# A streaming encoder's two layers on one core: four gate chunks by high and low parts, and an earlier order around the sample's attention and the experts' first quad

## The chip, the cores and the metric

The kernel runs on one core of one Trainium2 chip. The metric is the device time of a launch in microseconds, here the median of three runs. Profiles are single executions; their times count from the first instruction.

## What is computed

Two layers over 288 tokens of 1024 features in fp32: 256 of a prompt and 32 of a sample with a cache of earlier keys. Of each layer (cut):

```python
z = x @ w_in                       # [rnn | q | k | v | rnn gate | attn gate]
y_rnn = rglru(conv(z_rnn))         # linear recurrence over the tokens
o = attention(rope(q), rope(k), v) # banded for the prompt, cache for the sample
merged = sigmoid(z_gr) * (y_rnn @ w_br_rnn) + sigmoid(z_ga) * (o @ w_br_attn)
x = layernorm(alpha * x + merged @ w_out)
eidx, gate = route(x)              # 8 of 64 experts for each token
x = layernorm(alpha * x + shared(x) + sum(gate_e * expert_e(x)))
```

## The kernel before, in words

Activations lie with features on partitions (8 groups of 128, `xT`), tokens along the free dimension. The product with `w_in` goes by chunks of 128 output features; two chunks share a weight piece of 1 MB. A chunk is made in one of two ways. `over_features` (L563, matmuls L569) multiplies fp32 by fp32, 8 matmuls of 288 columns, two records each in the trace. `over_parts` (L572) has both operands split into a high and a low part of a reduced fp32 type and adds three products for each of 8 groups (L582, L583, L584), 24 matmuls. The low times low product is left out. The parts of activations are made once; those of a weight piece are made by ScalarE (`high_parts`, L1069: two copies into `whi`, which has two buffers) and VectorE (`low_parts`, L1409: two subtractions into `dense_lo`). `SPLIT` lists the pieces that are treated so, in order. Pieces go through a ring of three slots (`dense`); SyncE asks for piece d when piece d-3 is used, and puts transfers of the first quad's expert weights between them (`EXPERTS_AFTER`).

Work items are numbered (`Z_RNN` to `Z_FILL2`). Items before the gates use six PSUM banks in turn, from the gates on two. Each has two semaphores by parity: `z_ready`, set by TensorE, and `z_free`, set when the item was read out. `bank_of` (L555) waits before TensorE writes an item's bank: an item from the gates on waits until all earlier items of its parity are free.

TensorE's order in a layer: 8 chunks of the recurrence's input; k and v; 8 query chunks (items 10, 13, ..., 31), each with two block products of the recurrence's gates (L695; items 32 and 33 belong to the last). ScalarE turns the halves of each query chunk (L1129, four copies) and applies two sigmoids (L1153); VectorE makes the rotation (L1504, L1505, L1507). Behind query chunks 1 and 3 both also make parts of later pieces. Then come 16 gate chunks (items 34 to 49), spread over the attention by hand:

- `GATES_AHEAD`: chunk 0; transposes of the last keys and the sample's scores (L722 to L735); chunk 1; the sample's transposes (L743, L744), which wait for its softmax; the first pair's scores (L713, L714); chunks 2 and 3; the sample's output (L756, L757), which waits for ScalarE's copies of the transposed probabilities; chunk 4.
- `GATES_WITH`: for each of 8 pairs of heads, scores of the next pair, gate chunks, output of the pair before (`pair_output`, L771 to L773), transposes of this pair's probabilities (L791).

The chunks 0 to 7 go by `over_features` (pieces 9 to 12), 8 to 15 by `over_parts` (pieces 13 to 16). ScalarE reads each chunk out with a Tanh (`keep_gates`, L1162). Between, ScalarE makes the sample's exponentials (L1169), eight Exp (L1177) and eight Tanh (L1182) for the recurrence, the copies of the sample's probabilities (L1188, L1189), one Sqrt (L1193, a table load before and one after), and the exponentials of a pair (L1203). VectorE: maxima of the sample's scores (L1541), the product of gate and input (L1548), the sample's normalisation (L1534), squares (L1553, L1554), masked scores of the first pair (L1562 to L1566), memsets and the product and scan of the recurrence (L1573 to L1579), then the first pair's normalisation (L1534).

After the layer norm, the routed experts go in 16 quads of four. Before the first quad's turning TensorE makes the shared expert's last product (`shared_down`, L871, 8 chunks in two banks) and waits until VectorE has added its last chunk (L1792). Then come the turning of the hidden values (L920), slots to tokens (L942), and the gather of the next quad (L892 to L895), which needs the next one-hot matrix (L1722, VectorE). VectorE makes that behind the last sum.

## Time and profile before

| what | value |
|---|---|
| median of 3 runs | 1590.09 us (1589.77 to 1591.45) |
| profiled execution, its own time | 1589.3 us |
| its span | 1587.5 us |
| TensorE matmul busy | 1550.0 us (98%) |
| TensorE weight load busy | 1034.5 us (65%) |
| VectorE, ScalarE busy | 741.5 us (47%), 573.9 us (36%) |
| granted TensorE clock, mean | 0.997 |
| HBM read | 474.88 MB, 300 GB/s over the span |

A busy TensorE is one with a matmul under way, not one at its peak. The layers are alike: layer 0's gates lie at 82 to 175 us, its experts at 285 to about 800, layer 1's gates at 866 to 956, its experts from 1069 on. A row of an order of time has the start, the duration (of a merged group, from its first start to its last end), engine, line, operation, tiles, partitions x elements, count, and in brackets how long the engine had been idle and who released it.

### The profile page before, as it was taken

What the parts mean: (1) busy time and instruction counts of PE and PEld (TensorE: products, weight loads), DVE (VectorE), ACT (ScalarE), POOL (GpSimd) and SP (SyncE); (2) the same over time, 40 slices, a digit from 0 to 9 for tenths busy, and PEclk for the clock granted to TensorE, in tenths of its full rate; (3) what the DMA queues carried; (4) which work ended last, traced back from release to release, by engine and by line L of the source; (5) the groups of instructions that cost most, each with busy time, mean ns of one, the idle gap of its engine ahead of it and who ended that gap; (6) DMA issues with size and microseconds to landing.
All of it is one profiled execution on the core that took longest, in us unless ns stands there. A gap on an engine that the chain in (4) does not pass through costs nothing.

```text
span 1587.5 us, 25312 instructions
## 1 busy us (share of the span) xinstructions
PE 1550.0 (98%) x9446; PEld 1034.5 (65%) x9446; DVE 741.5 (47%) x1513; ACT 573.9 (36%) x1108; POOL 25.0 (2%) x40
## 2 busy tenths in 40 slices
PE   7999999999999999999999999999999999999996
PEld 7968997655655565555598699975565555556554
DVE  5768667332433333233474776562243333324335
ACT  5756433222232232223267664342223223222322
POOL 2000000000000000000010000000000000000000
PEclk9999999999999999999999999999999999999998
DMA  8552446599999999999546424458999999999991
GB/s 235 188 209 85 134 160 245 212 372 409 410 399 402 401 417 401 403 404 402 206 127 232 153 91 153 147 212 322 401 404 398 408 404 416 400 404 407 401 407 45
DMA packets 141557, 477.38 MB, mean 301 GB/s; under 512 B 10020, under 2 KB 74084, under 8 KB 108724
## 3 DMA queue, kind: packets, MB, share of 16 engines
q1 hardware_dynamic: 139728, 473.50, 77.0%
q0 software_dynamic: 1408, 2.85, 0.7%
q8 instruction: 44, 0.72, 0.2%
q10 hardware_dynamic: 356, 0.13, 0.0%
q14 instruction: 21, 0.17, 0.0%
HBM read 474.88 MB, written 1.57 MB: 300 GB/s over the span
## 4 chain that ended last, share of the span: by engine, by line
PE 92%; DVE 5%; ACT 2%; issue 1%; DMA 0%; SPq 0%; DVEq 0%; ACTq 0%
PE ps L910 28%; PE ps L933 14%; PE ps L582 6%; PE ps L583 6%; PE ps L584 6%; PE ps L569 6%; PE ps L954 4%; PE ps L955 4%; PE ps L893 4%; PE ps L892 4%; PE ps L895 2%; PE ps L942 1%; PE ps L871 1%; PE ps L920 1%; PE ps L1004 1%
## 5 line engine op out<-in xcount | busy, mean ns | idle before, releaser
L910 PE MATMUL ps<-experts,xg 128*64 128x512 f32 x2048 | 445.0, 592 | 0.0
L910 PEld LDWEIGHTS ps<-experts,xg 128*64 128x64 f32 x2048 | 146.9, 137 | 291.5 <-issue 290.6
L582 PE MATMUL ps<-parts 128*128 128x288 f32 x768 | 232.4, 303 | 1.1 <-DVE dense_lo L1409 0.4
L933 PE MATMUL ps<-experts,hid 128*64 128x512 f32 x1024 | 226.8, 595 | 0.4 <-ACT hid L1283 0.4
L584 PE MATMUL ps<-parts,dense_lo 128*128 128x288 f32 x768 | 226.1, 294 | 0.0
L1749 DVE SCALAR_TENSOR_TENSOR yl<-ps,gsl,yh 128x512 fp32r<-128x512 f32 x128 | 96.1, 751 | 254.8 <-ACT yh L1291 254.8
L1737 DVE TENSOR_TENSOR hid<-ps,hid 128x256 f32<-128x256 f32 x64 | 27.2, 425 | 378.6 <-ACT hid L1278 378.6
L1278 ACT ACTIVATE hid<-ps 128x256 f32<-128x256 f32 x64 | 24.6, 385 | 404.8 <-PE ps L910 404.8
L933 PEld LDWEIGHTS ps<-experts,hid 128*64 128x64 f32 x1024 | 71.6, 137 | 131.9 <-issue 127.9
L1270 ACT ACTIVATE xg<-ps,gperm_all 128x256 f32<-128x256 f32 x256 | 130.8, 562 | 71.5 <-PE ps L895 71.5
L582 PEld LDWEIGHTS ps<-parts 128*128 128x128 f32 x768 | 144.3, 188 | 4.8 <-issue 2.3
L584 PEld LDWEIGHTS ps<-parts,dense_lo 128*128 128x128 f32 x768 | 144.5, 188 | 0.0
L892 PE MATMUL ps<-oh,xh 128*128 128x256 f32 x512 | 136.4, 288 | 0.0
L1291 ACT ACTIVATE yh<-ps,gsl 128x512 fp32r<-128x512 f32 x128 | 88.1, 688 | 128.8 <-PE ps L933 128.8
L893 PE MATMUL ps<-oh,xl 128*128 128x256 f32 x512 | 133.5, 282 | 0.0
L954 PE MATMUL ps<-ohT,yh 128*128 128x288 f32 x480 | 132.2, 305 | 0.0
L955 PE MATMUL ps<-ohT,yl 128*128 128x288 f32 x480 | 129.1, 295 | 0.0
L1409 DVE TENSOR_TENSOR dense_lo<-dense,parts 128x1024 fp32r<-128x1024 f32 x96 | 113.2, 1221 | 19.4 <-ACT parts L1069 19.4
L569 PE MATMUL ps<-xT,dense 128*128 128x288 f32 x448 | 112.6, 409 | 4.4 <-ACT B L1153 2.7
L1756 DVE TENSOR_TENSOR ffT<-ps,ffT 128x288 f32<-128x288 f32 x240 | 109.6, 456 | 15.4
L583 PE MATMUL ps<-parts 128*128 128x288 f32 x384 | 113.3, 295 | 0.0
L1069 ACT ACTIVATE parts<-dense 128x1024 fp32r<-128x1024 f32 x96 | 96.1, 1052 | 42.3 <-PE ps L584 41.7
(287 smaller groups left out, 1964.0 us busy)
## 6 DMA issues: line engine op xcount, KB each, us to landing
experts<-in_w SPq DMA_DIRECT2D x384, 1024.0 KB, 10.0
dense<-in_w_in SPq DMA_DIRECT2D x34, 1024.0 KB, 5.5
dense<-in_w_br_rnn SPq DMA_DIRECT2D x8, 1024.0 KB, 5.3
dense<-in_w_br_attn SPq DMA_DIRECT2D x8, 1024.0 KB, 5.2
dense<-in_w_out SPq DMA_DIRECT2D x8, 1024.0 KB, 5.2
dense<-in_ws SPq DMA_DIRECT2D x6, 1024.0 KB, 5.5
tok<-in_x_prompt SPq DMA_DIRECT2D x1, 1024.0 KB, 5.7
out_y_prompt<-tok SPq DMA_DIRECT2D x2, 512.0 KB, 2.6
```

The costliest lines, as they stand in the source:

```text
L569: last = mm(bank[:, 0:n], w[:, k, col:col + P], rhs(k), start=k == 0, stop=k == KC - 1)
L582: mm(bank[:, 0:T], w_hi[:, k, col:col + P], hi[:, k, :], start=k == 0, stop=False)
L583: mm(bank[:, 0:T], w_hi[:, k, col:col + P], lo[:, k, :], start=False, stop=False)
L584: last = mm(bank[:, 0:T], w_lo[:, k, col:col + P], hi[:, k, :], start=False, stop=k == KC - 1)
L892: mm(o, xh[:, t, x], oh[:, t, :], start=t == 0, stop=False)
L893: mm(o, xl[:, t, x], oh[:, t, :], start=False, stop=False)
L910: last = mm(ps[e % 2 * CAP:(e % 2 + 1) * CAP, UP[u], :], xg[:, k, e * CAP:e * CAP + CAP], experts[:, e, 0:2, k * DE:k * DE + DE], start=k ...
L933: last = mm(ps[e % 2 * CAP:(e % 2 + 1) * CAP, DOWN[u][b], :], hidT[:, u, m, e % 2 * CAP:(e % 2 + 1) * CAP], experts[:, e, 2, m * D + b * 5 ...
L954: mm(o, yh[:, u, c * P:c * P + P], ohT[:, u, :], start=u == 0, stop=False)
L955: last = mm(o, yl[:, u, c * P:c * P + P], ohT[:, u, :], start=False, stop=u == 1)
L1270: last = activation(xg[:, k, :], ps[:, SWAP[j], k % 2 * 256:k % 2 * 256 + 256], ACT.Identity, bias=gperm_all[:, L, 1, k:k + 1], scale=gper ...
L1409: V.tensor_tensor(low[:, x], slot[:, x], as_f(whi[:, f % 2, x]), ALU.subtract).then_inc(wlo_ready, 1)
```

## The change

Pieces 9 and 10 (`D_G`, `D_G + 1`) join `SPLIT`, so gate chunks 0 to 3 go by parts too. ScalarE and VectorE make their parts behind query chunks 5 and 7. Chunk 2 moves from behind the sample's transposes to ahead of them. Chunk 0 waits for item 30, the last one in its own bank, and no longer for item 32. ScalarE keeps chunk 0 ahead of the sample's exponentials, chunk 1 behind them, chunk 2 behind the eight Exp. The last chunk, 15, is made in two halves: groups 0 to 3 before the output of pair 6, groups 4 to 7 behind the transposes of pair 7, and it is kept behind the copies of pair 7's probabilities. Behind the shared expert, the wait for the last sum moves behind turning and slots to tokens (`shared_added`), and VectorE makes quad 1's one-hot before the eight sums.

```diff
--- before.py
+++ after.py
@@ -97,7 +97,7 @@
 RING = 3
 
 
-SPLIT = list(range(D_IN + 1, D_KV + 1)) + list(range(D_Q, D_G)) + list(range(D_G + 4, D_ROUTER))
+SPLIT = list(range(D_IN + 1, D_KV + 1)) + list(range(D_Q, D_G + 2)) + list(range(D_G + 4, D_ROUTER))
 F_Q = SPLIT.index(D_Q)
 F_G = SPLIT.index(D_G + 4)
 F_BR = SPLIT.index(D_BR)
@@ -110,7 +110,7 @@
 EXPERTS_AFTER = (D_G, D_G + 2, D_G + 4, D_ROUTER + 2, D_ROUTER + 2, D_ROUTER + 2)
 
 
-GATES_AHEAD = ((0, 1), (2, 3), (4,))
+GATES_AHEAD = ((0, 1, 2), (3,), (4,))
 
 GATES_WITH = ((5, 6), (7,), (8,), (9, 10), (11,), (12, 13), (14,), (15,))
 H_WITH = 2
@@ -558,7 +558,10 @@
 
                 if Z_DEEP <= i < Z_GATE:
                     pe.wait_ge(z_free[i % 2], z_count(L, i - Z_DEEP) + 1)
-                elif i >= Z_GATE:
+                elif i == Z_GATE:
+
+                    pe.wait_ge(z_free[i % 2], z_count(L, Z_GATE - Z_GATE % Z_DEEP) + 1)
+                elif i > Z_GATE:
                     pe.wait_ge(z_free[i % 2], z_count(L, i))
                 return ps[:, z_bank(i), :]
 
@@ -569,12 +572,12 @@
                     last = mm(bank[:, 0:n], w[:, k, col:col + P], rhs(k), start=k == 0, stop=k == KC - 1)
                 return last
 
-            def over_parts(L, bank, d, col, hi, lo, ready=None):
+            def over_parts(L, bank, d, col, hi, lo, ready=None, ks=range(KC)):
 
                 f = SPLIT.index(d)
                 w_hi = whi[:, f % 2, :].rearrange("p (k c) -> p k c", k=KC)
                 w_lo = dense_lo[:, d % RING, :].rearrange("p (k c) -> p k c", k=KC)
-                for k in range(KC):
+                for k in ks:
                     if col == 0 and k % 4 == 0:
                         pe.wait_ge(wlo_ready, (L * len(SPLIT) + f) * 2 + (k // 4 + 1))
                     if ready:
@@ -695,7 +698,7 @@
                         mm(bank_of(L, i)[:, 0:U], wax[:, j, c, :], u_[:, c, :], start=True, stop=True).then_inc(z_ready[i % 2], 1)
                 def gate_chunks(ms):
                     for m in ms:
-                        if m >= KC:
+                        if D_G + m // 2 in SPLIT:
                             over_parts(L, bank_of(L, Z_GATE + m), D_G + m // 2, m % 2 * P, x_hi, x_lo).then_inc(z_ready[m % 2], 1)
                             continue
                         if m % 2 == 0:
@@ -773,6 +776,12 @@
                         last = mm(ps[lo:hi, 6, 0:P], v[:, 0, kv], pt[:, 2 * P:3 * P], start=True, stop=True)
                     last.then_inc(s_o, 1)
 
+                def last_gate(ks):
+                    m = 2 * KC - 1
+                    if ks[0] == 0:
+                        bank_of(L, Z_GATE + m)
+                    return over_parts(L, ps[:, z_bank(Z_GATE + m), :], D_G + m // 2, m % 2 * P, x_hi, x_lo, ks=ks)
+
                 for c in range(KC):
                     n = L * (KC + 1) + c + 1
 
@@ -780,7 +789,10 @@
                         gate_chunks(GATES_WITH[c])
                     if c < KC - 1:
                         pair_scores(c + 1)
-                    if c > 0:
+                    if c == KC - 1:
+                        last_gate(range(KC // 2))
+                        pair_output(c - 1)
+                    elif c > 0:
                         gate_chunks(GATES_WITH[c][:1])
                         pair_output(c - 1)
                         gate_chunks(GATES_WITH[c][1:])
@@ -790,6 +802,7 @@
                         for k in range(3):
                             last = transpose(ps[:, 4 + h, k * P:k * P + P], S[:, c % 2, h, k * P:k * P + P], ident)
                     last.then_inc(s_pT, 1)
+                last_gate(range(KC // 2, KC)).then_inc(z_ready[(2 * KC - 1) % 2], 1)
                 pair_output(KC - 1)
 
 
@@ -870,6 +883,8 @@
                         for m in range(ME):
                             last = mm(bank[:, 0:T], w[:, m, c * P:c * P + P], hs[:, m, :], start=m == 0, stop=m == ME - 1)
                         last.then_inc(z_ready[c % 2], 1)
+
+                def shared_added():
                     for b in range(2):
                         pe.wait_ge(z_free[b], z_count(L, Z_SH2 + KC))
 
@@ -955,7 +970,7 @@
                             last = mm(o, yl[:, u, c * P:c * P + P], ohT[:, u, :], start=False, stop=u == 1)
                         last.then_inc(c_full, 1)
 
-                def quad(n, first=False, last=False):
+                def quad(n, first=False, last=False, after=None):
                     if not first:
                         up(n, 0)
                         up(n, 1)
@@ -963,6 +978,8 @@
                     turn(n)
                     slots_to_tokens(n, 0)
                     slots_to_tokens(n, 1)
+                    if after:
+                        after()
                     if not last:
                         gather(n + 1, n)
                     down(n, 0)
@@ -974,7 +991,7 @@
                     up(q, 1)
                     if meanwhile:
                         meanwhile()
-                    quad(q, first=True)
+                    quad(q, first=True, after=shared_added if meanwhile else None)
                     with pe.Fori(1, NQUAD - 1) as i:
                         quad(q + i)
                     if meanwhile:
@@ -1152,7 +1169,7 @@
                         bank = z_item(L, i)
                         activation(dst[:, c, :], bank[:, 0:U], ACT.Sigmoid, bias=prm_all[:, L, b * KC + c:b * KC + c + 1])\
                             .then_inc(z_free[i % 2], 1)
-                    if c in (1, 3):
+                    if c % 2:
                         high_parts(L, F_Q + 2 + c // 2)
                 def keep_gates(ms):
 
@@ -1162,6 +1179,8 @@
                         activation(dst, bank[:, 0:T], ACT.Tanh, scale=0.5).then_inc(z_free[m % 2], 1)
 
 
+                act.wait_ge(xc_used, L + 1)
+                keep_gates(GATES_AHEAD[0][:1])
                 act.wait_ge(s_max, L * (KC + 1) + 1)
                 for h in range(2):
                     for a in range(2):
@@ -1169,14 +1188,14 @@
                         activation(S[:, 0, h, a * 160:a * 160 + 160], ps[:, 2 + h, a * 160:a * 160 + 160], ACT.Exp,
                                    bias=ats[:, 0, 1, x:x + 1], scale=SCALE, accum_out=ats[:, 0, 2, x:x + 1])
                 activation(ats[:, 0, 4, :], ats[:, 0, 3, :], ACT.Exp).then_inc(s_exp, 1)
+                keep_gates(GATES_AHEAD[0][1:2])
                 act.wait_ge(gxu, L + 1)
                 for b in range(2):
                     act.wait_ge(z_free[b], z_count(L, Z_GATE))
                 act.wait_ge(decay_set, 1)
                 for c in range(KC):
                     activation(a_[:, c, :], gl_[:, c, :], ACT.Exp, scale=c8[:, 0, L, c:c + 1]).then_inc(act_own, 1)
-                act.wait_ge(xc_used, L + 1)
-                keep_gates(GATES_AHEAD[0])
+                keep_gates(GATES_AHEAD[0][2:])
                 act.wait_ge(act_own, (L + 1) * KC)
                 for c in range(KC):
                     activation(gl_[:, c, :], gl_[:, c, :], ACT.Tanh, scale=c8[:, 1, L, c:c + 1]).then_inc(a_and_t, 1)
@@ -1217,12 +1236,14 @@
                         keep_gates(GATES_WITH[c])
                     if c < KC - 1:
                         exponentials(c + 1)
-                    if c > 0:
+                    if 0 < c < KC - 1:
                         keep_gates(GATES_WITH[c])
                     act.wait_ge(s_pT, n + 1)
                     act.wait_ge(s_o, L * (KC + 1) + max(c, 1))
                     activation(PTa[:, w, 0, :], ps[:, 4, 0:3 * P], ACT.Copy)
                     activation(PTa[:, w, 1, :], ps[:, 5, 0:3 * P], ACT.Copy).then_inc(s_pT_kept, 1)
+                    if c == KC - 1:
+                        keep_gates(GATES_WITH[c])
                     if c in HIGH_WITH:
                         high_parts(L, F_G + HIGH_WITH.index(c))
 
@@ -1512,7 +1533,7 @@
                         decay_rates()
                     if L == 0 and c == 5:
                         sink_tables()
-                    if c in (1, 3):
+                    if c > 0 and c % 2:
                         low_parts(L, F_Q + 2 + c // 2)
                 dve.wait_ge(out_rows, 2 * L + 1)
                 V.tensor_copy(k_rows[:, 0, :], ps[:, 7, 0:P])
@@ -1755,11 +1776,11 @@
                         dve.wait_ge(c_full, FREE + n * KC + (c + 1))
                         V.tensor_tensor(ffT[:, c, :], ps[:, SWAP[c % len(SWAP)], 0:T], ffT[:, c, :], ALU.add).then_inc(c_added, 1)
 
-                def quad(n, i, first=False, last=False, hidden_made=False):
-                    if not last:
+                def quad(n, i, first=False, last=False, made=False):
+                    if not last and not made:
                         dve.wait_ge(og_ready, n + 1)
                         one_hot(n + 1, i + 1)
-                    if not hidden_made:
+                    if not made:
                         hidden(n, 0)
                         hidden(n, 1)
                     if not first:
@@ -1786,6 +1807,8 @@
                         V.tensor_tensor(hs[:, m, :], ps[:, 6 + m, 0:T], hs[:, m, :], ALU.mult).then_inc(sh_hid, 1)
                     hidden(q, 0)
                     hidden(q, 1)
+                    dve.wait_ge(og_ready, q + 1)
+                    one_hot(q + 1, 1)
 
                     for c in range(KC):
                         bank = z_item(L, Z_SH2 + c)
@@ -1803,7 +1826,7 @@
                     gated(q, 0)
                     if first:
                         meanwhile()
-                    quad(q, 0, first=True, hidden_made=first)
+                    quad(q, 0, first=True, made=first)
                     with dve.Fori(1, NQUAD - 1) as i:
                         quad(q + i, i)
                     V.tensor_scalar(rank[:, :, :], rank[:, :, :], -float(CAP), None, ALU.add).then_inc(next_round, NQUAD)
```


## Rows read from the trace of the kernel before

**Rows 1.** TensorE's waits over the span: total us, times, longest us

```profile
PE ps L569 <- ACT B L1153: 2.7, 2, 1.4
PE ps L743 <- DVE S L1534: 2.5, 2, 1.3
...
PE ps L920 <- DVE ffT L1792: 1.5, 2, 0.8
```

**Rows 2.** TensorE in order of time, layer 1: start, duration, [idle before <-releaser]

```profile
865.97 4.12 PE L569 MATMUL ps<-xT,dense 128*128 128x288 f32 x16 [1.37 <-ACT B L1153]
...
871.48 4.15 PE L569 MATMUL ps<-xT,dense 128*128 128x288 f32 x16
876.89 0.33 PE L743 MATMUL ps<-cst,S 128*128 128x128 f32 x1 [1.27 <-DVE S L1534]
...
879.59 8.00 PE L569 MATMUL ps<-xT,dense 128*128 128x288 f32 x32 [0.74 <-ACT B L1162]
```

**Rows 3.** Order of time, layer 1, last pair, TensorE and VectorE

```profile
955.11 0.43 PE L771 MATMUL ps<-PTa,v 128*64 128x128 f32 x2 [0.96 <-ACT PTa L1225]
...
949.04 1.01 DVE L1534 TENSOR_SCALAR S<-S,ats 128x256 f32<-128x256 f32 x4
```

**Rows 4.** Chain that ended last, layer 1, gate chunks 4 to 6

```profile
890.46 11.84 PE ps L569 x48
```

**Rows 5.** A stretch, L582 alone: PE busy (x), PEld busy (x), clock

```profile
957.00:989.00 32.00, 23.80 (x81) 15.03 (x81) 1.00 0.41 133
```

**Rows 6.** Order of time, layer 0, one piece's high and low parts

```profile
68.35 2.00 ACT L1069 ACTIVATE parts<-dense 128x1024 fp32r<-128x1024 f32 x2
...
69.51 2.36 DVE L1409 TENSOR_TENSOR dense_lo<-dense,parts 128x1024 fp32r<-128x1024 f32 x2 [0.79 <-ACT parts L1069]
```

**Rows 7.** SyncE's DMA issues in order of time, layer 1

```profile
855.32 8.71 SPq L446 DMA_DIRECT2D dense<-in_w_in  x2
```

**Rows 8.** The page's DMA issues: count, KB each, median us to landing

```profile
dense<-in_w_in SPq DMA_DIRECT2D x34, 1024.0 KB, 5.5
```

**Rows 9.** ScalarE in order of time, layer 1

```profile
863.66 1.64 ACT L1129 ACTIVATE tmp<-ps 32x288 f32<-32x288 f32 x4 [1.34 <-PE ps L584]
...
865.99 0.50 ACT L1153 ACTIVATE B<-ps,prm_all 128x291 f32<-128x291 f32 x1 [0.15 <-DVE qT L1504]
...
875.61 3.54 ACT L1177 ACTIVATE B<-B,c 128x291 f32<-128x291 f32 x8 [0.80 <-DVE B L1548]
...
879.63 3.53 ACT L1182 ACTIVATE B<-B,c 128x291 f32<-128x291 f32 x8
883.06 0.37 ACT L1188 ACTIVATE PTa<-ps 128x256 f32<-128x256 f32 x1
```

**Rows 10.** VectorE in order of time, layer 1

```profile
871.59 0.89 DVE L1541 TENSOR_REDUCE ats<-ps 128x2 f32<-128x320 f32 x2 [0.69 <-PE ps L735]
...
872.99 2.58 DVE L1548 TENSOR_TENSOR B<-B 128x2328 f32<-128x2328 f32 x1
...
891.56 0.07 DVE L1573 MEMSET B<- 128x8 f32 x1 [1.86 <-ACT B L1193]
...
900.45 1.01 DVE L1534 TENSOR_SCALAR S<-S,ats 128x256 f32<-128x256 f32 x4
```

**Rows 11.** Order of time, layer 0, VectorE and TensorE

```profile
78.36 0.46 DVE L1504 TENSOR_TENSOR qT<-ps,cst 128x288 f32<-128x288 f32 x1
...
82.65 0.48 PE L569 MATMUL ps<-xT,dense 128*128 128x288 f32 x1 [1.37 <-ACT B L1153]
```

**Rows 12.** Order of time, layer 1, shared expert, TensorE and VectorE

```profile
1083.06 8.03 PE L871 MATMUL ps<-hs,dense 128*128 128x288 f32 x32
...
1084.33 0.46 DVE L1792 SCALAR_TENSOR_TENSOR ffT<-xT,ps 128x288 f32<-128x288 f32 x1 [0.32 <-PE ps L871]
...
1091.76 0.96 DVE L1722 TENSOR_TENSOR oh<-cst,rank 128x768 fp32r<-128x768 f32 x1 [0.19 <-DVE ffT L1792]
```

**Rows 13.** The span's end: busy PE, PEld, DVE, ACT, POOL; clock, DMA

```profile
1576.00:1587.50 11.50, 0.00 (x0) 0.00 (x0) 8.72 (x14) 2.06 (x3) 0.00 (x0) 0.57 0.27 103
```

## The prediction, made before the change was run

> **What bounds the kernel now.** I read the waits of TensorE first, then its order of time in layer 1, then ScalarE and VectorE beside it, then the same places of layer 0. TensorE is the bound: it waits for others for a few microseconds only, and the places that the change touches are among them [rows 1]: the first gate chunk behind a sigmoid (2.7 us over both layers), the sample's transposes behind its softmax (2.5), the first token work of the experts behind a sum (1.5). Layer 1 adds 0.74 us in front of gate chunk 2 [rows 2] and 0.96 in front of the last pair's output [rows 3]. So an instruction taken from TensorE, or a wait taken away, counts in full, as long as ScalarE and VectorE keep up.
>
> **Part 1, four chunks split.** A gate chunk by fp32 takes 11.84/3 = 3.95 us (the stretch of chunks 4 to 6) [rows 4]. A chunk by parts is 24 matmuls, 8 of them of L582; 81 of these in 32.0 us [rows 5] make 0.395 us for each three and 3.2 us for a chunk. So 0.75 us a chunk, 3.0 a layer. That time comes from the rows. The Trainium skill (FP8 and Floating Point Precision, TensorE Precision Notes) says that a true fp32 matmul goes through the array in four passes; three passes would then be 2.96 us, and the eight chunks together would give 1.9 us more than by my rows. This case's rows have 0.81 of the fp32 time, not 0.75, and the sum goes by them.
>
> The price is paid by ScalarE, 2.00 us of high parts for each of two weight pieces, and VectorE, 2.36 us of low parts, the second half ending 3.5 us after ScalarE's begin [rows 6]. They lie behind query chunks 5 and 7. The later of the two pieces (10) is asked for at 855.32 in layer 1 and read by ScalarE from 866.4 on, 11 us later, where such a transfer lands in 5.5 us as a median [rows 7, 8]; so I put no wait there.
>
> **Part 2, the start and the front, layer 1.** The chunk at 865.97 waits 1.37 us for the sigmoid of chunk 7. By the new rule it needs the second one of chunk 6, over before the rotation of chunk 7 begins, so it follows L695 at once, at 864.5 (865.97 - 1.37, a tenth less for overlap). ScalarE has 1.34 us of idle time before the rotation of chunk 7 [rows 9], which takes the delay by the first high parts (0.6 us there). The chunk ends at 867.7; kT's transposes and the sample's scores, 1.5 us (871.48 - 865.97, less 4.0 for the chunk) [rows 2], end at 869.2, 2.3 us earlier than now.
> Then the second high parts: they begin 0.4 us after the sigmoid of 865.99, at 866.4, and VectorE's low parts end at 869.9 [rows 6, 9]. Behind them on VectorE are queued the copy of the key rows (0.5 us) and the sample's maxima. These begin at 870.3 for 871.59; the wait for scores has become one for low parts. Everything of that chain is 1.3 us earlier: gx·u begins at 871.7 for 872.99 [rows 10], and ScalarE's eight exponentials at 874.3. Between these and the eight Tanh it now keeps one gate chunk and not two (0.3 us), so the Tanh begin 1.6 us earlier, at 878.05, and the copies of the sample's probabilities 1.6 earlier, at 881.45 [rows 9]. Four of them take 1.2 us, so TensorE can multiply them at 882.65.
> TensorE meanwhile: chunks 1 and 2 from 869.2 to 875.6; transposes and first pair's scores 875.6 to 877.6 (876.89 to 878.85 now, L743 to the wait before 879.59) [rows 2]; chunk 3 to 880.8. The waits of 1.27 and 0.74 us are gone, and a **new one of 1.85 us** stands before the sample's output, 882.65. Its 2.9 us (879.59 + 8.00 to 890.46) and chunks 4 to 6 with 11.84 follow unchanged [rows 2, 4]: 902.3 becomes 897.5. **Gain 4.8 us.**
> Next on the path could be the first pair's softmax. Today its last multiplication ends at 901.46, 9.9 us behind the memset at 891.56 [rows 10], which waits for a Sqrt that waits for gate chunk 3. With chunk 3 kept early, the Sqrt waits only for VectorE's squares, which move with the Tanh, 1.6 us; the masked scores before the memset end at 888.1, and the softmax at 898.0. TensorE wants it at 897.5 + 0.9 = 898.4. So it is hidden, by 0.4 us only. If the table load before Sqrt (1.3 us) can't start ahead of the wait, 0.5 us a layer is lost.
>
> **The same in layer 0.** VectorE also sets the sink tables behind query chunk 5, until chunk 6's product with cosine at 78.36 [rows 11]. The low parts begin there and end at 80.65, and that product waits for them. ScalarE's sigmoid ends at 81.6, and the first gate chunk begins at 81.75 for 82.65 [rows 11]: 0.9 us for the 1.5 above. Its last sigmoid ends at 84.5 for 83.16, the high parts at 86.4, the low parts at 87.85, and gx·u begins at 89.7, as today. So the Tanh gains just the 0.3 us of one chunk less; TensorE resumes with the sample's output at 100.65 instead of 104.2. **Gain 3.5 us**, and the margin before the softmax is 0.4 us again, since the Sqrt no longer waits for a gate chunk.
>
> **Part 3, the last chunk in halves.** Today TensorE stands for 0.96 us between the transposes (end 954.15) and the last pair's output [rows 3]. Half a chunk, 1.6 us, now lies there and covers ScalarE's two copies (0.5 us each). The total of TensorE's work stays. The transposes come 1.6 us earlier and need the last softmax at 951.6; its multiplications end by 950.05 today [rows 3]. ScalarE's keeping of chunk 15 and the high parts behind it come later against the work, yet o's high and low parts end at 961.1, and piece 18 is due at 961.9. The piece that waits for chunk 15's slot is due 14 us later. **Gain 0.96 a layer, 1.9.**
>
> **Part 4, the one-hot ahead of the sums.** The 0.75 us before L920 [rows 1] goes: turning and slots run while the last sum is added, and the gather's wait is met behind them. But VectorE now makes the one-hot, 0.96 us [rows 12], between the hidden products and the first sum, which moves from 1084.33 to 1084.9 and ends at 1085.35, while TensorE wants that bank at 1085.1 (two chunks of 8.03/8 = 1.0 us behind 1083.06). That is a new wait of 0.3 to 0.4 us. **Gain 0.4 a layer, 0.8**; the ends are 0 and 0.75.
>
> **Sum.** 4.8 + 3.5 + 1.9 + 0.8 = 11.0 us. The experts' stage has no wait of TensorE for a weight and only moves. The profiled execution takes 1589.3 us, which would be 1578.3. The median of the runs stands 0.8 us above it, so the same gain gives **1579.1 us**.
>
> **Bounds.** Upwards in gain: layer 0 like layer 1 (+1.3) and no stall in part 4 (+0.7): 1577.1; another microsecond if the chain to the Tanh is a little shorter: 1576. Downwards: 0.5 a layer for the table load, a microsecond a layer on the ScalarE and VectorE chains (nothing in the trace shows high parts between Sigmoid and the sample's Exp), none of part 4: 1.0 + 2.0 + 0.8 = 3.8, 1583. The instructions of part 2 on TensorE can't cost less than their rows.
>
> **Rivals.**
> *The helpers' chain sets the front* (chance 0.20). If ScalarE and VectorE slip by 2 to 3 us in each front, because copies and subtractions are in the way of rotations and sigmoids as in layer 0's decay rates, the new wait grows from 1.85 to 4 or more and half the front's gain (4.2) is gone: 1579.1 + 4.2 = 1583.3. For it: the margins before the first pair's softmax are 0.4 us. Against it: ScalarE has 1.34 us to spare before a rotation in layer 1 [rows 9].
> *The parts come late* (0.05). The chunk waits for piece 9 or 10, which were not read before so early; a transfer later by 4 to 5 us in each layer would eat the 8.3 of the front and leave 2.7: 1587.4, within 0.2% (what a measurement of this kernel can tell from no change, 3.2 us). Against it: piece 10 is asked for 11 us before use [rows 7].
> *The clock falls in the new wait* (0.03). This is the one that ends slower. In the last 11.5 us, where TensorE is idle, the granted clock is 0.57 [rows 13]; today waits of 1.4 us leave it at 1.00. The new wait of 1.85 us is the longest inside the layers, with transposes close before it. If the clock went to 1.2 of 2.4 GHz there and came back only at the end of chunk 6, the 14.8 us of work after it [rows 4] would take 14.8 more in each layer: 29.6 - 11.0 = 18.6 slower, 1608.7. It decides from 7.1 us a layer on ((11.0 + 3.2)/2). The Trainium skill speaks for this direction (TensorE: Matmul & The Clock Gate, HAM oscillation): short bursts with waits between them send the array back to half clock each time. The trace so far agrees only at the end of the kernel, and disagrees around every wait inside it, so the chance is small.
> *It does not do what it says* (0.02): the halves or the early start change nothing because another count of the same semaphore holds; only part 1 stays, 6.0 less the new wait's 3.7: 1587.8.
>
> **How the numbers follow.** My forecast has 0.70. The range takes its bounds and the nearer half of the first rival: 1576 to 1583.5. Faster by over 0.2%: the forecast and the first rival, 0.90; within it the late parts and the change without effect, 0.07; slower the clock, 0.03.
>
> **What would show it.** Right: L569's first wait gone and layer 1's gate chunk within 0.2 us of L695; a wait of about 1.8 us before L756, with ScalarE as releaser; no wait before the last L771; L920 straight behind L871 and a wait of 0.3 inside L871; L1548 at the same time as before in layer 0 and 1.3 us earlier in layer 1. Wrong: a wait for L1534 behind chunk 6, one of L582 for low parts in the first gate chunks, or a granted clock below 1.00 between the layers' fronts and chunk 6.

## The result, and the profile after

Five runs of the kernel after have a median of **1580.72 us** (1580.43 to 1584.69), five of the kernel before beside them 1590.09 (1588.79 to 1591.45): a ratio of 0.9945, 95% interval 0.9931 to 0.9960. It is faster by 9.4 us. The forecast was 1579.1 in a range of 1576.0 to 1583.5; 11.0 us of gain were expected. The profiled execution took 1580.72 us itself, with a span of 1578.8.

The span's start varies by some microseconds between executions (the wait for the sample's input alone is 7.1 to 8.6 us). So I compare a stretch behind it: from the block products of query chunk 4 in layer 0, at 66.55 here, to the first quad's turning in layer 1, at 1083.17. I call it the **stretch**. It was 1024.9 us before and is 1016.6 after, 8.3 less; with 0.4 us from its start that is the whole difference of the spans, 8.7.

First the waits of TensorE over the span of the kernel after (total us, times, longest us). The three rows of before [rows 1] are gone but for 0.3 us before the sample's transposes and 0.5 us before the first gate chunk, both in layer 0. In their place stands a new one, ahead of the sample's output.

```profile
PE ps L599 <- DMA tok<-in_x_sample: 7.4, 1, 7.4
PE ps L759 <- ACT PTa L1208: 3.6, 2, 1.8
...
PE ps L585 <- ACT B L1170: 0.5, 1, 0.5
...
PE ps L746 <- DVE S L1555: 0.3, 1, 0.3
```

TensorE in order of time, layer 1: start, duration, and in brackets the idle time and who ended it. The first gate chunk stands directly behind the block products and no longer waits [rows 2], chunks 1 and 2 take 6.5 us, and the sample's transposes wait for nothing.

```profile
859.66 1.14 PE L698 MATMUL ps<-B,wax 128*128 128x291 f32 x4
860.42 0.51 PE L585 MATMUL ps<-parts 128*128 128x288 f32 x1
...
865.37 0.40 PE L585 MATMUL ps<-parts 128*128 128x288 f32 x1
...
871.87 0.27 PE L746 MATMUL ps<-cst,S 128*128 128x128 f32 x1
...
873.70 0.40 PE L585 MATMUL ps<-parts 128*128 128x288 f32 x1
...
878.88 0.40 PE L759 MATMUL ps<-PTa,vc_all 128*64 128x128 f32 x2 [1.72 <-ACT PTa L1208]
```

The chain that ended last has gate chunks 4 to 6 behind that, in layer 0 and in layer 1. They took 11.84 us before [rows 4].

```profile
103.26 13.53 PE ps L572 x48
...
881.80 13.51 PE ps L572 x48
```

The same 48 records are 1.7 us longer. Why, the windows of layer 0 show (start:end, us, then busy time and count of PE, PEld, DVE, ACT, POOL, the granted clock, DMA share, GB/s): TensorE is busy throughout, and its granted clock is 0.53 in the third one.

```profile
96.00:100.00 4.00, 2.50 (x19) 2.26 (x17) 3.27 (x5) 4.00 (x12) 0.00 (x0) 1.00 0.10 9
100.00:103.30 3.30, 2.97 (x17) 1.62 (x18) 3.16 (x5) 2.07 (x4) 0.00 (x0) 1.00 0.97 328
103.30:106.70 3.40, 3.40 (x8) 2.44 (x9) 3.19 (x11) 3.12 (x2) 0.00 (x0) 0.53 1.03 405
106.70:110.00 3.30, 3.30 (x14) 2.52 (x14) 3.23 (x3) 0.94 (x4) 0.00 (x0) 0.97 0.50 200
```

In layer 1 the window 882.0 to 885.3 has 0.52. In the same place before, every window has 1.00; this one is of layer 1:

```profile
890.50:902.30 11.80, 11.80 (x50) 9.00 (x50) 9.65 (x15) 4.94 (x13) 0.00 (x0) 1.00 0.84 299
```

ScalarE and VectorE, layer 1, in order of time. The table load of L1212 begins behind the kept chunk, 2.5 us before its Sqrt, and the first pair's last multiplications end at 894.07.

```profile
879.05 1.28 ACT L1212 ACT_TABLE_LOAD   x1
881.55 2.14 ACT L1212 ACTIVATE B<-B 128x2328 f32<-128x2328 f32 x1 [1.22 <-DVE B L1575]
```

```profile
867.80 2.58 DVE L1569 TENSOR_TENSOR B<-B 128x2328 f32<-128x2328 f32 x1
...
893.06 1.01 DVE L1555 TENSOR_SCALAR S<-S,ats 128x256 f32<-128x256 f32 x4
```

Last, the end of the attention and the shared expert, TensorE in layer 1. The last pair's output follows the second half of chunk 15 with no wait, where 0.96 us stood before [rows 3], and the turning L935 stands directly behind the shared product, which is 8.33 us long for 8.03 [rows 12].

```profile
947.06 0.43 PE L774 MATMUL ps<-PTa,v 128*64 128x128 f32 x2
...
1075.00 8.33 PE L884 MATMUL ps<-hs,dense 128*128 128x288 f32 x32
1083.17 0.60 PE L935 MATMUL ps<-cst,hid 128*128 128x128 f32 x4
```

Cut at the same points, the two traces give (us, layer 0 / layer 1):

| stretch | before | after | difference |
|---|---|---|---|
| block products of chunk 4 to the sample's output | 37.25 / 36.55 | 33.79 / 31.72 | -3.46 / -4.83 |
| to the second pair's scores | 14.72 / 14.72 | 16.38 / 16.36 | +1.66 / +1.64 |
| to the last pair's output | 52.88 / 52.88 | 51.83 / 51.82 | -1.05 / -1.06 |
| to the first quad's first product | 114.06 / 114.06 | 114.05 / 114.05 | 0 |
| to the turning | 22.65 / 22.68 | 22.05 / 22.05 | -0.60 / -0.63 |

The turning of layer 0 to chunk 4 of layer 1, 542.5 us, is the same in both.

### The profile page after: what moved, and what is told of

Read it like the earlier page. It is cut to its first block, busy times and chain, and to the rows that moved or that the text cites. A ratio compares the mean times of both kernels' runs of the same rounds, so it can differ in the third digit from the quotient of the medians.

```text
span 1578.8 us, 25460 instructions
## 1 busy us (share of the span) xinstructions
PE 1548.1 (98%) x9510; PEld 1038.9 (66%) x9510; DVE 750.7 (48%) x1521; ACT 581.1 (37%) x1116; POOL 25.0 (2%) x40
## 4 chain that ended last, share of the span: by engine, by line
PE 90%; DVE 5%; ACT 2%; issue 1%; DMA 0%; SPq 0%; DVEq 0%; ACTq 0%
PE ps L925 28%; PE ps L948 14%; PE ps L585 6%; PE ps L586 6%; PE ps L587 5%; PE ps L969 4%; PE ps L572 4%; PE ps L970 4%; PE ps L907 4%; PE ps L908 4%; PE ps L910 2%; PE ps L957 1%; PE ps L884 1%; PE ps L935 1%; DVE dense_lo L1430 1%
## 5 line engine op out<-in xcount | busy, mean ns | idle before, releaser
L585 PE MATMUL ps<-parts 128*128 128x288 f32 x832 | 252.1, 303 | 1.5 <-ACT B L1170 0.5
L587 PE MATMUL ps<-parts,dense_lo 128*128 128x288 f32 x832 | 244.9, 294 | 0.0
L585 PEld LDWEIGHTS ps<-parts 128*128 128x128 f32 x832 | 156.3, 188 | 6.1 <-issue 2.2
L587 PEld LDWEIGHTS ps<-parts,dense_lo 128*128 128x128 f32 x832 | 156.5, 188 | 0.0
L1430 DVE TENSOR_TENSOR dense_lo<-dense,parts 128x1024 fp32r<-128x1024 f32 x104 | 122.6, 1221 | 23.3 <-ACT parts L1086 23.2
L586 PE MATMUL ps<-parts 128*128 128x288 f32 x448 | 132.2, 295 | 0.0
L1086 ACT ACTIVATE parts<-dense 128x1024 fp32r<-128x1024 f32 x104 | 104.0, 1051 | 42.4 <-PE ps L587 36.2
L969 PEld LDWEIGHTS ps<-ohT,yh 128*128 128x128 f32 x480 | 90.2, 188 | 24.3 <-issue 24.3
```

What stands on the lines that cost most here:

```text
L585: mm(bank[:, 0:T], w_hi[:, k, col:col + P], hi[:, k, :], start=k == 0, stop=False)
L586: mm(bank[:, 0:T], w_hi[:, k, col:col + P], lo[:, k, :], start=False, stop=False)
L587: last = mm(bank[:, 0:T], w_lo[:, k, col:col + P], hi[:, k, :], start=False, stop=k == KC - 1)
L969: mm(o, yh[:, u, c * P:c * P + P], ohT[:, u, :], start=u == 0, stop=False)
L1430: V.tensor_tensor(low[:, x], slot[:, x], as_f(whi[:, f % 2, x]), ALU.subtract).then_inc(wlo_ready, 1)
```

## The experiments

Diffs are against the kernel after unless said otherwise. "Front" is the first line of the table above, "tail" the second, which holds the small products of the sample's output (2.9 us) and gate chunks 4 to 6.

### The clock behind the wait

The theory: the clock falls because TensorE stands idle for 1.8 us. The rival: the products by parts ahead of it count for less. First, useless products fill the wait (`keep_clock`, a helper that both kernels use at two other places; here two fp32 products of 512 columns of a constant, into the bank that the sample's output overwrites next).

```diff
                 gate_chunks(GATES_AHEAD[1])
+                keep_clock(6, 2)
```

> The changed kernel with two fp32 products of 128x512 without use (about 0.85 us each) in the new wait before the sample's output; nothing else. Theory A: the granted clock fell to 0.50 for 3.4 us in each layer because TensorE stood 1.84 us. Then the clock stays at 1.00, chunks 4 to 6 take 11.84 us again and not 13.5, and the time is 1.7 us a layer less: about 1577.3 us. Theory B: the clock falls for another cause (the small products of the sample's output, or the products by parts ahead of them). Then it falls as before and the time stays at 1580.7 us.

Measured: 1578.41 us (1577.34 to 1580.55, 5 runs), ratio to before 0.9928 (0.9914 to 0.9941). The stretch is 1013.3, 3.3 less than after, and the front is the same within 0.05 us: the fillers (1.88 us) lie where the wait was. The windows of its layer 0:

```profile
98.20:100.20 2.00, 1.94 (x6) 0.63 (x4) 1.93 (x3) 2.00 (x8) 0.00 (x0) 1.00 0.27 32
100.20:103.10 2.90, 2.82 (x16) 1.51 (x16) 2.76 (x5) 1.67 (x3) 0.00 (x0) 1.00 1.02 353
103.10:115.00 11.90, 11.90 (x51) 9.07 (x50) 11.52 (x21) 5.94 (x13) 0.00 (x0) 1.00 0.67 242
```

So the fall hangs on the wait, and it costs 3.3 us in this execution. One filler leaves 1.0 and 0.9 us of the wait:

```diff
+                keep_clock(6, 1)
```

> The changed kernel with one useless product of 0.85 us in the wait instead of two; about 1.0 us of wait is left. Theory A, by the kernel before, whose waits of 1.37 us left the clock at 1.00: no fall, chunks 4 to 6 take 11.84 us, S is 1013.3 as with two. Rival: a wait of any length behind small products is enough, the clock falls and S is 1016.6.

1582.71 us (1580.46 to 1584.61, 4 runs), ratio 0.9945 (0.9927 to 0.9964), stretch 1016.4. The clock fell again, in both layers (layer 0):

```profile
103.00:107.00 4.00, 3.03 (x18) 1.53 (x17) 3.83 (x6) 2.76 (x7) 0.00 (x0) 0.95 0.91 279
107.00:110.50 3.50, 3.50 (x9) 2.56 (x9) 3.29 (x11) 3.08 (x2) 0.00 (x0) 0.56 1.03 407
```

That is a miss for length as the cause: before, waits of 1.37 and 1.27 us leave the clock at 1.00, and in split_only below one of 2.66 us does. The next kernel makes the wait longer, without new products by parts: pieces 9 and 10 by fp32, chunk 3 behind the wait.

```diff
-SPLIT = list(range(D_IN + 1, D_KV + 1)) + list(range(D_Q, D_G + 2)) + list(range(D_G + 4, D_ROUTER))
+SPLIT = list(range(D_IN + 1, D_KV + 1)) + list(range(D_Q, D_G)) + list(range(D_G + 4, D_ROUTER))
-GATES_AHEAD = ((0, 1, 2), (3,), (4,))
+GATES_AHEAD = ((0, 1, 2), (), (3, 4))
```

with `c in (1, 3)` in both helpers as before.

> No chunk of the first four by parts (as in no_split), and gate chunk 3 moved behind the sample's output, so that a wait of some 2.3 us stands there again though no product by parts is new. Stretch S from the block products of query chunk 4 in layer 0 to the first quad's turning in layer 1: 1024.9 us before, 1016.6 changed, 1013.8 no_split. Theory A (the wait makes the clock fall): it falls in both layers, S is 1013.8 + 4.6 of waits + 3.4 of slow clock, 1021.8. Rival (products by parts make it fall): the clock stays at 1.00 and S is 1018.4.

1593.81 us (1589.7 to 1597.14, 10 runs), ratio 1.0022 (1.0010 to 1.0034), stretch 1026.2: slower than before. The wait is 3.3 us in each layer, and the clock is at half for twice as long:

```profile
97.50:100.80 3.30, 2.21 (x8) 1.05 (x8) 3.16 (x5) 2.22 (x5) 0.00 (x0) 0.70 0.00 0
100.80:104.50 3.70, 3.70 (x12) 2.07 (x12) 3.46 (x12) 3.23 (x2) 0.00 (x0) 0.50 0.01 2
104.50:108.00 3.50, 3.50 (x14) 2.69 (x13) 3.43 (x3) 0.20 (x1) 0.00 (x0) 0.84 0.00 0
```

The expectation was missed by 4.4 us: with 2.3 us of wait and 1.7 of slow clock a layer, the stretch was to be 1021.8. The waits are 1.0 us longer each, and the slow clock costs 2.9 and 3.0. The profiled execution is the fastest of the ten; the others have a mean granted clock of 0.993 down to 0.991, so the loss in them is as large or larger.

The rival is out as a condition: the clock falls without a single new product by parts, if behind a longer wait than in the kernel after. And in layer 0 the half clock already begins at 98.8, only 0.2 us behind the start of the sample's output (98.58): 0.70 over the first window is 2.0 us at half. So there the small products behind the wait can't be what brought the clock down.

Two kernels keep the wait out of the place by real work. In the one, gate chunk 4 goes ahead of the sample's output:

```diff
+                gate_chunks(GATES_AHEAD[2])
                 pe.wait_ge(s_pT_kept, L * (KC + 1) + 1)
...
-                gate_chunks(GATES_AHEAD[2])
```

> The changed kernel with gate chunk 4 ahead of the sample's output, so that real work lies in the new wait. Theory A: no wait of TensorE and no fall of the clock there; of the 3.5 us a layer that this frees (1.84 of wait, 1.7 of slow clock) the first pair's softmax lets about 2.1 through and takes the rest as a wait behind chunk 6 of 1.3 us: about 1576.4 us. Theory B (clock falls for another cause): the fall remains, and the time is 1.8 us a layer less at most, with no wait for the softmax: 1577 to 1578 us.

1578.85 us (1576.41 to 1579.80), ratio 0.9922 (0.9909 to 0.9936), stretch 1012.1, no wait before the output and the clock at 1.00. But it gives back 1.3 and 1.2 us: the first pair's transposes now wait 1.4 to 1.5 us for its softmax, as the row of its waits shows (two of the four are the 0.5 us that every kernel here has at a later pair):

```profile
PE ps L802 <- DVE S L1554: 3.8, 4, 1.5
```

The other keeps the wait, where it was, and makes chunk 4 between the wait and the sample's output:

```diff
                 pe.wait_ge(s_pT_kept, L * (KC + 1) + 1)
+                gate_chunks(GATES_AHEAD[2])
...
-                gate_chunks(GATES_AHEAD[2])
```

> The kernel after, but TensorE waits for the last sample's kept probabilities (s_pT_kept) first, then makes gate chunk 4 (dense, 3.9 us), and only then the small products of the sample's output. The wait of about 1.84 us stays at its place in the order; what stands right behind it is dense work in place of the 2.9 us of small products. Theory C (the clock falls where a wait stands directly beside the small products of the sample's output, and they fill the time behind it): the granted clock stays at 1.00, chunks 4 to 6 take their 11.84 us of work in place of 13.5, nothing is lost behind the wait, the stretch from layer 0's fifth block group to layer 1's first turning is 1013.3 us (1016.6 less 3.3), and the time some 1577.5 to 1579.5. Rival (a wait of 1.84 us at this place is enough, whatever follows): the wait is 1.8 again, the clock falls to 0.50 for 3.4 us or more in both layers, the stretch is 1016.6 (1018 to 1020 where it is low for 6.8 us), the time 1580.5 to 1584.5 as for the kernel after.

1579.84 us (1577.88 to 1581.18, 5 runs), ratio 0.9933 (0.9920 to 0.9947), stretch 1013.6. The wait is there and the clock does not fall. First TensorE's row, then the windows of layer 0:

```profile
101.55 4.12 PE L572 MATMUL ps<-xT,dense 128*128 128x288 f32 x16 [1.79 <-issue]
```

```profile
99.70:101.60 1.90, 0.10 (x2) 0.08 (x1) 1.83 (x3) 1.90 (x7) 0.00 (x0) 1.00 0.37 33
101.60:105.70 4.10, 4.10 (x17) 2.98 (x18) 3.93 (x7) 2.86 (x3) 0.00 (x0) 1.00 1.03 370
105.70:108.60 2.90, 2.90 (x17) 1.53 (x18) 2.73 (x9) 2.87 (x6) 0.00 (x0) 1.00 1.03 410
```

A wait of the same length at the same moment, the same small products 4 us later, and 3.0 us are saved. So, for a wait of this length, it is neither the wait nor the small products alone, but the two side by side. That rests on two fronts in one trace, and on the mean granted clocks below.

### What the split is worth

Without the two pieces (`SPLIT` and the helpers as before, the order of the kernel after kept):

> The changed kernel with pieces 9 and 10 left as one fp32 product each, so gate chunks 0 to 3 take 3.95 us again; start, order, halves and one-hot stay. Theory A: four times 0.75 us more work fill the wait before the sample's output, the clock stays at 1.00, and without parts the helpers start 0.3 to 1.3 us earlier. The front then gains 3.8 us in each layer against the kernel before, and the time is 1578 us: the split of four chunks is worth nothing or less. Rival (what the prediction's sum said, no clock): the split is worth 3.0 us a layer less the wait of 1.85, so without it the time is 1 to 2 us more than 1580.7: 1582 to 1583 us.

1579.20 us (1578.92 to 1582.09), ratio 0.9932 (0.9919 to 0.9946), stretch 1013.8: **less than with the split**, by 2.8 us. TensorE has some 5.4 us more to do (in layer 1 the front less its waits is 32.67 us for 30.0, so 2.7 a layer and not the 3.0 of the rows), and no wait stands before the sample's output. The front is 33.37 / 32.67, so 0.4 shorter in layer 0 and 0.95 longer in layer 1; the rest is the clock, which stays at 1.00.

The split alone, on the kernel before (pieces 9 and 10 in `SPLIT`, `D_G + m // 2 in SPLIT`, parts behind all odd query chunks):

> The kernel before with the four chunks by parts and nothing else (order, start, last chunk and one-hot as before). By rows 3.0 us a layer less work. Theory A: ScalarE's and VectorE's chain holds back the sample's transposes, a wait of 2 to 3 us stands before them, and only 2.4 us of layer 1 and 1.6 of layer 0 arrive; if the clock falls behind these waits, 1.7 a layer goes again. S 1020.9 to 1024.3 of 1024.9. Rival (the prediction's term as it stands): S 1018.9.

1588.23 us (1586.26 to 1589.58, 10 runs), ratio 0.9985 (0.9975 to 0.9994), stretch 1021.8, 3.1 less than before. Of the 5.4 us by which TensorE's work is shorter, 2.6 come back as longer waits at the two first places of [rows 1]:

```profile
PE ps L582 <- ACT B L1153: 3.9, 2, 2.7
PE ps L743 <- DVE S L1534: 3.9, 2, 2.0
```

And the clock: in layer 1, where the second of these waits stands at 876.99 (1.95 us) and another 0.64 us at 879.58, it is 1.00 in every window. In layer 0 it is 1.00 as well, around waits of 2.66 us (before the first gate chunk, by parts), 1.96 and 0.65.

```profile
872.00:880.00 8.00, 5.41 (x42) 4.71 (x41) 4.76 (x12) 6.01 (x20) 0.79 (x2) 1.00 0.70 250
880.00:889.00 9.00, 9.00 (x63) 7.51 (x62) 7.98 (x12) 7.29 (x16) 0.00 (x0) 1.00 0.16 37
```

Only piece 9 split, in the order of the kernel after:

```diff
-... list(range(D_Q, D_G + 2)) ...
+... list(range(D_Q, D_G + 1)) ...
-                    if c % 2:
+                    if c in (1, 3, 5):
```

> The changed kernel with piece 9 split (gate chunks 0 and 1) and piece 10 not. Theory A: TensorE needs 1.5 us more than with four chunks by parts, so the wait before the sample's output shrinks to 0.3 us or nothing and the clock stays at 1.00; gain of the front 5.2 us in layer 1 and 4.7 in layer 0: about 1576 us. Rival (no cost of the clock in the wait): the work of 1.5 us fills the wait and the time stays at 1580.7 us.

1579.36 us (1577.18 to 1580.21), ratio 0.9932 (0.9918 to 0.9945), stretch 1012.0: the shortest with chunk4_ahead. TensorE does not wait before the sample's output (0.48 us stand before layer 0's first gate chunk), and yet that output begins earlier than in the kernel after (front 32.74 / 31.29). The reason is on VectorE: without the low parts of piece 10 its product of gate and input begins 21.17 / 19.72 us behind the block products of chunk 4, for 22.71 / 20.64 after. VectorE and TensorE (layer 1):

```profile
864.66 2.58 DVE L1569 TENSOR_TENSOR B<-B 128x2328 f32<-128x2328 f32 x1
```

```profile
849.10 1.14 PE L698 MATMUL ps<-B,wax 128*128 128x291 f32 x4
...
876.23 0.43 PE L759 MATMUL ps<-PTa,vc_all 128*64 128x128 f32 x2
```

### The three other parts, each undone

The first gate chunk waits for item 32 again (`elif i >= Z_GATE`, no case of its own):

> The changed kernel, but gate chunk 0 again waits for all earlier items of its parity (the sigmoid of query chunk 7). Theory A: TensorE starts 0.9 us later in layer 0 and 1.5 later in layer 1, the wait before the sample's output shrinks by as much to under 1 us, the output itself moves by 0 and 0.5 us, and the clock does not fall: S is 1016.6 - 3.4 + 0.5 = 1013.7, so the early start costs more than it brings here. Rival (no tie of the clock to the wait): S is 1017.1, or 1019.0 where the start was on the path in full.

1583.77 us (1582.79 to 1584.17, 4 runs), ratio 0.9954 (0.9937 to 0.9970), stretch 1017.7. The front is 34.41 / 32.36, so the early start is worth 0.62 and 0.64 us. The expected stretch was 1013.7, with no fall of the clock behind so short a wait; that is missed. The wait before the sample's output is 0.8 us in both layers. In layer 0 the clock holds (tail 14.69), in layer 1 it falls, for twice as long as after, and the tail is 17.94:

```profile
881.00:884.40 3.40, 3.40 (x17) 1.71 (x17) 3.26 (x6) 2.18 (x2) 0.00 (x0) 0.79 0.86 280
884.40:888.00 3.60, 3.60 (x8) 2.60 (x9) 3.39 (x10) 2.53 (x2) 0.00 (x0) 0.50 1.05 408
```

The last gate chunk whole, as before:

```diff
-                    if c == KC - 1:
-                        last_gate(range(KC // 2))
-                        pair_output(c - 1)
-                    elif c > 0:
+                    if c > 0:
-                last_gate(range(KC // 2, KC)).then_inc(z_ready[(2 * KC - 1) % 2], 1)
```

> The changed kernel with the last gate chunk in one piece ahead of pair 6's output and kept where it was. By theory and by the prediction's part 3 the wait of 0.96 us before the last pair's output is back in both layers and S grows by 1.9 to 2.1 us to 1018.6. Rival: the halves only moved the wait (into the transposes of pair 7 or into the branch products), S grows by under 1 us.

One run, 1587.26 us (before beside it 1591.53), stretch 1020.1. The part up to the last pair's output is 52.86 in both layers for 51.83: the halves are worth **1.05 us a layer**. The other 1.4 us are the clock's: with the same instructions in the front, it fell for twice as long in layer 1 (tail 17.83).

The wait for the last sum and the one-hot as before:

```diff
-                    quad(q, first=True, after=shared_added if meanwhile else None)
+                    quad(q, first=True, after=None)
-                    dve.wait_ge(og_ready, q + 1)
-                    one_hot(q + 1, 1)
```

> The changed kernel with the wait for the last sum inside the shared product and the next one-hot behind the sums, as before. Expected: 0.6 us a layer more from the first up product to the turning (22.65 for 22.05), S 1017.8; the stall of 0.3 us inside the shared product is gone.

One run, 1586.28 us, stretch 1019.3. Up to the turning it takes 22.65 for 22.05: **0.6 us a layer** by both parts together; the remaining 1.5 us are again a longer fall, in layer 0 this time (tail 17.97). And the late wait kept, the one-hot behind the sums again:

> The changed kernel with the late wait for the last sum kept, but the next one-hot behind the sums. Expected: the turning comes 0.9 us earlier than before, but the gather then waits some 0.3 to 0.5 us for the one-hot, so that its first product starts 23.6 us behind the first up product, where it is 23.7 in the kernel before and 23.2 in the changed one: the advance of the one-hot is what brings the gain. Rival: the one-hot's place does not matter, and the gather starts at 22.8 us, without the stall of 0.3 us.

One run, 1586.29 us, stretch 1018.3. The turning comes at 21.75, 0.3 earlier than after, since nothing delays the first sum (L884 takes 8.03). But then the gather waits, in both layers, and the layer between the turnings and the next block products is 543.30 for 542.52:

```profile
1087.73 0.60 PE L935 MATMUL ps<-cst,hid 128*128 128x128 f32 x4
1089.58 0.39 PE L907 MATMUL ps<-oh,xh 128*128 128x256 f32 x1 [0.60 <-DVE oh L1743]
```

Together 22.5 us, where before has 22.65 and after 22.05: moving the wait alone brings 0.15, the one-hot's place brings the rest.

## Why the prediction was right, and where it was not

**The front.** Forecast: 3.5 and 4.8 us. Measured: 3.46 and 4.83. The new wait was to be 1.85 us with ScalarE's copies as releaser; it is 1.84 and 1.72. Parts 1 and 2 hold in detail: no wait before layer 1's first gate chunk, 3.25 us a chunk by parts (3.2 by my rows, so 0.7 us saved a chunk for 0.75, which only shortens the new wait), 0.46 us of the wait left in layer 0, L1569 in layer 0 at its old place and no wait for a weight or for low parts. The Trainium skill's rule (FP8 and Floating Point Precision, TensorE Precision Notes), read as three passes in place of four, would have, as an estimate, 2.96 us for such a chunk; the trace does not agree.

**The margins behind it.** The table load did start ahead of its wait, so no 0.5 us was lost. The first pair's softmax was to end 0.4 us before it is wanted. It ends at 894.07, and the chunks before its use at 895.3 with 0.9 us of scores behind them: 2.1 us, of which 1.7 are the slower clock's. Chunk4_ahead shows how thin the rest is: it waits for just that softmax, and loses 1.3 and 1.2 us there.

**The halves.** Forecast 0.96 a layer, measured 1.05 (undo_halves).

**The one-hot and the sums.** Forecast 0.4 a layer with a stall of 0.3 to 0.4 in the shared product. The stall is 0.30 (8.33 less 8.03), and the gain 0.6. Without the wait the turning comes 0.90 us earlier (late_wait_only, 22.65 to 21.75), and not by the 0.75 of idle time that its row shows; less the stall that is 0.6.

**The step that failed** is the sentence of part 2 "Its 2.9 us and chunks 4 to 6 with 11.84 follow unchanged". They follow with 13.5, because the granted clock is at half behind the new wait. That is the rival that had a chance of 0.03, in kind though not in size. The prediction's own sign of being wrong, a granted clock below 1.00 between the fronts and chunk 6, is there. The rival was priced at 14.8 us a layer, as if the clock came back only at the end of chunk 6. It came back after 3.4 us, which costs 1.7 a layer, and in some executions after twice that, which costs 3.2. So two things were wrong: the chance, and the price, and the two hid each other. The sum by the measured terms is 3.46 + 4.83 - 3.30 + 2.11 + 1.23 = 8.3, where the forecast had 11.0; the 2.7 us between them are 3.3 of clock less 0.6 for the sums and the halves. The total then missed by 1.6 us only, since the profiled execution of after started 0.4 us earlier and its median does not stand above it, where the forecast added 0.8. That it lies in the range is partly luck: the 3.8 us allowed for a smaller gain stood for the table load, the helpers' chains and part 4, none of which took any of it, and the clock used 3.3.

The argument against the clock was "today waits of 1.4 us leave it at 1.00" [rows 1]. It compared lengths. What the runs show:

| kernel | wait, and what follows it | granted clock behind it |
|---|---|---|
| before | 1.3, transposes and scores (2.0), then 0.7 | 1.00 |
| before | 1.0, output of the last pair (1.1) | 1.00 |
| split_only | 2.0, transposes and scores, then 0.6 | 1.00 |
| split_only, undo_start | 2.7 in layer 0, a chunk by parts (3.2) | 1.00 |
| wait_then_chunk4 | 1.8, a dense chunk (4.1) | 1.00 |
| fill_wait, no_split, one_piece, chunk4_ahead | none, the sample's output | 1.00 |
| undo_start | 0.8, the sample's output | 1.00 in layer 0, 0.50 in layer 1 |
| fill_one | 1.0 and 0.9, the sample's output | 0.50 |
| after | 1.8 and 1.7, the sample's output | 0.50 |
| undo_halves, undo_sums, late_wait_only | 1.8 and 1.7, the sample's output | 0.50, in one layer of each for twice as long |
| chunk3_late | 3.3, the sample's output | 0.50, for twice as long |

The sample's output has 16 records of small products with 64 columns of weights, half of them on 32 partitions (L760). They keep TensorE busy in the records, and yet 0.8 us of idle time beside them can be enough (it was in one layer of two) where 2.0 us beside transposes is not. Of 14 fronts with a wait directly before them, 13 have a fall. Products with 64 columns of weights are not enough by themselves: in before, 0.96 us stand directly before the last pair's output, 12 such records of 1.1 us on 128 partitions, and the clock stays at 1.00 in both layers.

The other executions agree, by the mean granted clock that each has on record. It is 0.997 or 0.998 in all of before, no_split, one_piece, chunk4_ahead and wait_then_chunk4 and in four of fill_wait's five (the fifth 0.996); 0.994 to 0.996 in after, fill_one and undo_start; 0.991 to 0.993 in chunk3_late. Two falls of 3.4 us at half are 0.002 of the span. Nine of split_only's ten are at 0.997. The tenth is at 0.994: a fall can come there too.

The Trainium skill (TensorE: Matmul & The Clock Gate, HAM oscillation) tells of a kernel whose short bursts of matmuls stand between waits for DMA, and which goes back to half clock in each round. The trace of after agrees in direction, in both layers, with one wait of 1.8 us in work that is dense otherwise. How long a fall lasts goes with where it begins. Read from the traces in stretches of 0.5 us, the six falls that begin 0.2 to 2.2 us behind the start of the sample's output last 6.8 us, and the seven that begin 2.4 to 3.2 us behind it last 3.4.

**What stays open** is which property of these products counts, the 32 partitions, their length or the 64 columns with one of these, and why the fall begins now early and now late, or not at all, behind equal instructions (undo_start's two layers; undo_halves, undo_sums and late_wait_only have one layer of each length). So something outside the order of the instructions has a part in it, and a single trace at 1.00 does not show that a front is safe. It is probably also in the spread of after's own runs: the one of 1584.69 us has a mean granted clock of 0.994, the four of 1580.4 to 1580.7 have 0.995 or 0.996. Only the profiled one of them has a trace, so where the clock fell in the others is argued, not shown.

**What the change is worth by parts.** The halves bring 2.1 us, the sums 1.2, the early start 1.3 (measured with the split). The order of the front, the early start with it, brings most: no_split has it without the split, and its stretch is 11.1 us below before, 7.8 of them in the fronts (2.1 and 1.2 are the halves and the sums). The split, the largest piece of new work, brings nothing beside it: it takes 5.4 us off TensorE, and the sample's output does not come earlier for it than ScalarE and VectorE allow, so that the time comes back as a wait (3.6 us) and as clock (3.3). With the clock held up (fill_wait) it is worth 0.5 us. I had taken it in the forecast as a gain that the new wait "eats", correctly as a sum; I had not asked what the front would be without it.

**A better version.** One_piece and chunk4_ahead have stretches 4.6 and 4.5 us below after, and fill_wait, no_split and wait_then_chunk4 2.8 to 3.3 us, in one execution each. Their medians, 1578.4 to 1579.8, lie 0.9 to 2.3 us below after's 1580.72, and the intervals of the ratios overlap with after's: by the times none of them is told apart from after; the stretch is what speaks for them. One_piece is the one to keep: no wait before the sample's output, no filler, and half of the split's work on ScalarE and VectorE saved.

## What to carry to other kernels

Before you take work off the bound engine, ask what its next wait is for: if that is a chain of other engines, the work comes back as a wait, and taking those engines' extra work away (here the second piece's low parts) can move the end further than taking TensorE's. When a wait is left over, look at what stands beside it, not at its length alone: put a dense chunk there, and keep the small products in the middle of dense work. And compare a fixed stretch of two traces rather than two totals when the start of the span varies by as much as the effect.

## What the runs showed of the hardware that was not expected

- A wait of 0.8 to 1.8 us directly before 2.9 us of small products halved TensorE's granted clock in 11 of 12 fronts, for 3.4 or 6.8 us, which costs 1.7 or 3.2 us. A wait of 1.8 us before a dense chunk, of 2.7 us before a chunk by parts, or of 2.0 us before transposes and scores didn't in the traces taken.
- The fall began 0.2 to 3.2 us behind the end of the wait, and it lasted 6.8 us where it began within 2.2 us, 3.4 us where later (13 falls).
- The fall shows neither in the waits nor in the busy share (TensorE is 100% busy in the window with 0.53). It shows in the granted clock of a window and in a group of equal records that has become longer (13.53 us for 11.84).
- A table load of ScalarE starts before the semaphore that its own ACTIVATE waits for: 1.28 us at 879.05, for a Sqrt at 881.55 that then waits 1.22 us for VectorE.
